# Four expert weight loads on ScalarE's queue, issued at four later places instead of all together

## The reference

```python
h = layer_norm(DEEPNORM_ALPHA * x + mixed, ln1_g, ln1_b)      # mixed = (gates * branches) @ w_out
scores = sigmoid(h2d @ w_router)                               # 64 experts
eidx, ew = top 6 of the 4 best of 8 groups, weights normalised * 2.5
ffn = routed_experts(h2d, eidx, ew, w_exp_gate, w_exp_up, w_exp_down) \
    + swiglu(h2d, w_sh_gate, w_sh_up, w_sh_down)               # shared expert, 256 wide
y = layer_norm(DEEPNORM_ALPHA * h + ffn, ln2_g, ln2_b)
```

## Time and profile before

| what | value |
|---|---|
| median of three runs, no profiler | 1888.15 us |
| profiled execution, its time | 1905.46 us |
| profiled execution, span from first to last instruction | 1903.7 us |
| PE busy in the span | 1787.2 us (94%) |
| DVE, ACT, POOL busy | 690.5, 421.7, 352.0 us |
| mean granted TensorE clock | 0.974 |
| routed experts, gate and up product (L2355), busy | 471.2 us |
| routed experts, down product (L2346), busy | 246.0 us |

### The profile page before, as it was taken

One profiled execution on the slowest core, in us unless ns is written; L12 is line 12 of the kernel. 1 busy time (PEld: TensorE's weight loads), 2 busy tenths in 40 slices (PEclk: granted clock), 3 DMA queues, 4 the chain that ended last, 5 costly groups with the idle time before them and its releaser, 6 DMA issues. The chain is left out here.

```text
span 1903.7 us, 24449 instructions
## 1 busy us (share of the span) xinstructions
PE 1787.2 (94%) x8660; PEld 1226.5 (64%) x8660; DVE 690.5 (36%) x1482; ACT 421.7 (22%) x862; POOL 352.0 (18%) x288
## 2 busy tenths in 40 slices
PE   8999899999898998999987999999999999999990
PEld 8999899999654557988754444444445444445440
DVE  3112433443255555636764222222222222222224
ACT  3112122222444553111100011111111111111114
POOL 0000330430200000001056122212222222222213
PEclk9999999999989999999998999999999999999995
DMA  6331633442302217342251589999999999999966
GB/s 216 106 93 48 187 107 105 153 129 72 123 23 78 64 38 295 138 156 78 70 214 35 191 322 382 381 381 380 382 373 370 366 363 362 375 376 365 334 207 213
DMA packets 133019, 411.61 MB, mean 216 GB/s; under 512 B 17620, under 2 KB 79092, under 8 KB 115332
## 3 DMA queue, kind: packets, MB, share of 16 engines
q1 hardware_dynamic: 108418, 319.77, 44.7%
q0 software_dynamic: 21504, 73.87, 14.8%
q10 hardware_dynamic: 3026, 17.04, 2.2%
HBM read 339.11 MB, written 73.96 MB: 217 GB/s over the span
## 5 line engine op out<-in xcount | busy, mean ns | idle before, releaser
L2355 PE MATMUL e_G<-wb,pages 128*128 128x512 f32 x1072 | 471.2, 592 | 0.7 <-DMA wb<-in_w_exp_gu 0.3
L2355 PEld LDWEIGHTS e_G<-wb,pages 128*128 128x128 f32 x1072 | 203.5, 190 | 257.1 <-issue 257.1
L2346 PE MATMUL e_Y<-mixT,e_aT 128*128 128x512 f32 x544 | 246.0, 595 | 3.9 <-ACT e_aT L2217 1.8
L2188 POOL DMA_INDIRECT d_base<-e_y_sb,e_s_idx x68 | 107.7, 1584 | 585.3 <-DMA d_base<-e_y_sb,e_s_idx 538.7
L2346 PEld LDWEIGHTS e_Y<-mixT,e_aT 128*128 128x128 f32 x544 | 98.0, 190 | 103.0 <-issue 100.4
L1261 PE MATMUL gate_ps<-x_hi,gw_hi 128*128 128x352 f32 x464 | 151.7, 327 | 1.6 <-DVE r_srg L1067 1.6
L181 PE MATMUL ps<-w_hi,x_hi 128*128 128x244 f32 x512 | 143.4, 280 | 8.6 <-DVE x_lo L235 8.4
L1261 PE MATMUL gate_ps<-x_hi,gw_lo 128*128 128x352 f32 x464 | 149.6, 323 | 0.0
L1261 PE MATMUL gate_ps<-x_lo,gw_hi 128*128 128x352 f32 x464 | 149.1, 321 | 0.0
L181 PE MATMUL ps<-w_hi,x_lo 128*128 128x244 f32 x512 | 142.5, 278 | 0.0
L181 PE MATMUL ps<-w_lo,x_hi 128*128 128x244 f32 x512 | 142.3, 278 | 0.0
(11 more groups left out here) (410 smaller groups left out, 2716.4 us busy)
## 6 DMA issues: line engine op xcount, KB each, us to landing
wb<-in_w_exp_gu SPq DMA_DIRECT2D x64, 2048.0 KB
mixT<-in_w_exp_dn SPq DMA_DIRECT2D x68, 1024.0 KB
gw_sb<-in_w_gate SPq DMA_DIRECT2D x20, 512.0 KB, 6.7
d_proj<-o_sb SPq DMA_DIRECT2D x8, 1098.0 KB, 5.8
d_gateT<-r_g_out ACTq DMA_DIRECT2D x16, 528.0 KB, 2.7
pages<-in_cache_both SPq DMA_DIRECT2D x64, 128.0 KB, 2.0
wb<-in_w_exp_gu ACTq DMA_DIRECT2D x4, 2048.0 KB
w_sb<-in_w_in SPq DMA_DIRECT2D x7, 976.0 KB, 10.8
```

The costliest lines, as they stand in the source:

```text
L2188: g.indirect_dma_start(base, bass.IndirectOffsetOnAxis(ap=s_idx[s][:, 0:1], axis=0), y_sb[:, c, :], None, compute_op=ALU.add).then_inc(y_o ...
L2346: mm = t_.matmul(Y[q][:], aT[:, c, k, :], w_d[:, s, k, q * 512:(q + 1) * 512], start=k == 0, stop=k == 1)
L2355: mm = t_.matmul(G[c], xT[:, c, k, :], w_gu[s][:, :, k, :], start=k == 0, stop=k == KD - 1)
```

## The change

The four loads are taken out of the loop behind the wait for `y_done` and put, one by one, at four later places of ACT's stream. The wait itself stays where it was. The first load now stands behind the scores of the last tile, the second and third behind `gate(1)`, the fourth behind `gate(2)`. Nothing else is changed: sizes, buffers, semaphores and the other engines' code are the same.

```diff
             act.wait_ge(y_done, NT)
-            for s in range(4):
+
+            def first_weights(s):
                 act.dma_start(wb[s][:].rearrange("p q k n -> p (q k n)"), a["w_exp_gu"][s]).then_inc(gu_in[s], 16)
             evac(NT - 2)
             scores(NT - 3)
...
             evac(NT - 1)
             gate(0)
             scores(NT - 1)
+            first_weights(0)
             gate(1)
+            first_weights(1)
+            first_weights(2)
             gate(2)
+            first_weights(3)
             act.wait_ge(bk, BK_STEPS)
             act.dma_start(meta[0:P, :], meta_i[:]).then_inc(meta_out, 16)
```

## The result

The changed kernel took 1891.70 us (median of 22 runs, 1887.56 to 1899.33), the kernel before 1887.91 us beside it (22 runs, 1885.18 to 1894.99). The ratio is 1.0020, with an interval of [1.0011, 1.0028]: slower by 3.8 us. The forecast said no change; 1891.70 lies at the top of its range, and the sign is that of the rival with the chance of 0.13. One later execution (2838.59 us at a granted clock of 0.612, of the kernel with the fourth load in two halves) stands apart from all others and is left out of its ratio.

The account below looks back on a forecast made before the run. PE was taken as the bound nearly everywhere, so time counts only where PE waits. 1888.15 + 0 (issues) + 0 (arrival) - 0 (signal) = 1888.1 us, no change (0.58); range 1881.2 to 1892.0 us.

Parts of the forecast that it names:

- The list's load can't be hit: POOL's list load lands at 1043.4 us, PE asks at 1065.14 us; 12.3 us remain even without the stumble, more than a load.
- the stumble: At 1028 to 1042 us PE is busy only 4.61 of 14 us, with no weight load under way: 9.39 us lost.
- The slower rival: Fourth load at 1052 us pushes the gather of expert 0; PE waits, 1893.7 us, at most 8.85 us lost; chance 0.13.
- Its rule on the clock: Behind an idle stretch of PE the granted clock dips, partly 1.2 instead of 2.4 GHz, costing 2.10 us on 32 matmuls.
- The size of the load: One weight load on the DMA engines takes 5.2 us alone, 6.75 us with what ran beside the four.
- Issues 0 and arrival 0: On ACT's queue, four moved issues of 0.38 us fall in idle time; every load lands 39 us or more early: cost 0.
- The late signal, taken as 0: At 981 us PE's signal reaches ACT's sigmoid after 4.85 us; gain 0 to 6.91 us profiled, 0 chosen without the profiler.
- The sum that seemed to prove it: Signal 4.81, clock 2.10 and PE's gap at 1028 us 9.39 make 16.30 of the profiled execution's 17.31 us excess.
- The rule of 6.2 us: Cited against the forecast: a profile's total lies about 6.2 us above ordinary time, leaving about 11.1 us for both places.
- the late signal is real: Full DMA engines with POOL's scatters delay PE's signals even without a profiler; the change gives 1883.3 to 1881.2 us; chance 0.29.

Follow-up runs that it names:

- the calm execution: The kernel before itself, nothing changed, profiled once more in a last run on a fifth chip: a single execution of 1891.22 us.

## Why the prediction was wrong

- **"The list's load can't be hit"** is the step that failed. It said that 12.3 us remain between list and PE without the stumble. The runs showed 1.6 us, and a wait of 2.23 us with the fourth load in front. The rows are right, but they are those of a stumbling execution. Rows of the kernel before in the profile of the prediction, from the start of `gate_up(0)` over the half that stumbles to the first product of expert 0:

```profile
957.66 9.63 PE L2011 MATMUL e_T<-mixT,pages 128*128 128x352 f32 x32
...
1028.95 1.05 PE L2011 MATMUL e_G<-mixT,pages 128*128 128x352 f32 x3
...
1051.20 3.60 PE L2027 MATMUL m_T<-pages 128*128 128x512 f32 x8
...
1077.30 7.10 PE L2076 MATMUL e_G<-wb,pages 128*128 128x512 f32 x16 [0.33 <-ACT pages L1736]
```

  Counted from the first, POOL issues the list's load after 83.6 us there and after 82.2 us in the calm execution: the stumbles hardly touch POOL. PE asks for it after 107.5 and 87.9 us. So PE lost 19.6 us, 18.2 of them against POOL, of which I took off 9.4. The late signal and its dip were not taken off at all, and the stumble was larger than the window of the earlier trace rows shows: from 1028.95 to 1051.20 us PE takes 22.25 us for a half that takes 9.47 in the calm execution, 12.8 us more. The list itself lands 4.1 us after its issue and not 2.1. And I kept the fourth load where the stumbling ACT had it, at 1052 us and behind the list (1041.30). When nothing stumbles, `gate(2)` comes 8.1 us before the list's load (1034.91 and 1042.99), and the load stands in front of it.
- **The slower rival** had the right load and the wrong victim. It named the gather, priced at 5.5 us. The victim was the last scatters and, behind them, the list, at 2.23 + (5.40 - 3.70) = 3.9 us. Its rule on the clock held in kind: the dip behind the wait cost 1.7 us, where I took 2.10 from the earlier trace rows.
- **The size of the load**: 5.2 to 6.75 us from issue to landing became 12.9, with SP's stores and loads under way in the same 13 us (DMA share 0.99 in 1042 to 1051 us). "DMA: Bandwidth & Descriptors" of the Trainium skill, section "Issuing engines are not separate DMA queues", says that transfers of all issuers interleave on the same engines; the trace agrees (POOL's wait for its scatters 6.50 us without and 9.39 us with ACT's load beside them).
- **Issues 0 and arrival 0** held. The fourth load landed at 1050.5 us, long before its product.
- **The late signal, taken as 0** for the median, held in value: it is absent from the executions shown from calm chips, so there was nothing to win. The reason given does not hold: ten profiles from calm chips don't have it, so it is not the profiler's alone, and it goes with the scatters on some chips. The sum that seemed to prove it, 16.30 of 17.31 us, came out by luck. Its 9.39 us should have been 12.8, and the stage of that execution is 119.64 - 100.06 = 19.6 us longer than the calm one, more than the whole difference that it was to explain. The record does not say on which chip that execution ran.
- **The rule of 6.2 us**: the prediction cites "Runtime: NRT & Kernel Launch" of the Trainium skill, section "The ~15µs preamble/postamble breakdown", for a profile that lies about 6.2 us above the ordinary time. No such constant is seen here: the profiled executions of the kernels with six or more runs lie between 3.4 us below and 6.9 us above the medians (1906.37 beside 1909.74, 1898.57 beside 1891.70). It can't serve to split a gap of 17.31 us.
- **Rival "the late signal is real"** (0.29) fell: the signal was on time with the four loads and the scatters under way on a calm chip (DMA share 0.85), on time with the loads and no scatters on a stumbling one (0.91), and 4.60 us late where no load had been issued yet.

## What to carry to other kernels

When a profile's time differs from the median by more than the change can bring, its gaps can't just be subtracted: an engine that stalls comes late against those that don't, so every margin between two engines in that profile is too wide or too narrow by the stall. Take another profile, or measure margins from a common event on each engine's own pace. A load that is moved to be "out of the way" is to be checked against every small transfer that someone waits for within its length, above all those that wait for one another (scatters, then a list, then a gather): here 2 MB beside the last scatters and a list of 64 KB cost 4 us, since there was only 1.6 us to spare.

## What the hardware showed unexpectedly

The same program has a median of 1888, 1902 or 1911 us by the chip. In the longer ones PE's matmuls start some 2.8 us apart in a few stretches (1038.82, 1041.62, 1044.42 above) though nothing is missing, and signals between engines come up to 10.6 us late. Without the 54 scatters these are gone on the chip of 1911 us, and 22 us with them. Why one chip does this and another does not, no run shows.

The eight matmuls behind a wait at the list took 5.39 to 5.40 us in place of 3.70 us in three profiles (waits of 2.23, 2.35 and 2.74 us) and 5.65 us behind a wait of 5.01: here a wait of 2.23 us cost 3.9 us in all, and the slow group behind the longest wait added only 0.25 us more than behind the short ones.
